# Two retimings in a matmul-bound kernel: the causal heads' value products after the gates' tile, the dilated heads' transposes without a wait

## The reference, cut to what matters

```
(qa, ka, va, za, qb, kb, vb, zb, qm, zm, gates) = split(h @ w_in)
qa, ka = rope(qa), rope(ka)                    # 8 causal heads of width 128
ya = softmax(qa ka^T / sqrt(128), causal) va * silu(za)
qb, kb = rope(qb), rope(kb)                    # 4 dilated heads, 3 dilations each
yb = mixture over the 3 dilations * silu(zb)
ym = softmax(qm mk^T / 16) mv * silu(zm)       # 4 memory heads of width 256
```

## Time and profile before

| | |
|---|---|
| Median of 3 runs | 3493.75 us (3493.48 to 3502.49) |
| Profiled execution | 3492.97 us, of which the span is 3491.7 us |
| PE busy | 3264.7 us, 93% of the span, 20298 matmuls |
| DVE busy, ACT busy | 1738.8 us (50%), 1260.3 us (36%) |
| A chunk's transfer, issue to landing | 4.2 us, median of 936 |
| Causal heads, dilated heads, memory heads | about 2458 to 2619 us, 2619 to 2893 us, 2893 to 3018 us of the span |

### The profile page before, as it was taken

How to read it: one execution, slowest core, us unless ns; L and a number is a source line. 1 busy time by engine, 2 the same in 40 slices (tenths; PEclk the granted TensorE clock), 3 DMA queues, 4 the chain that set the end, 5 groups by cost and what they waited for, 6 DMA issues and landing times.

```text
span 3491.7 us, 47726 instructions
## 1 busy us (share of the span) xinstructions
PE 3264.7 (93%) x20298; PEld 2782.5 (80%) x20298; DVE 1738.8 (50%) x2491; ACT 1260.3 (36%) x1779; POOL 0.2 (0%) x4
## 2 busy tenths in 40 slices
PE   5979999999999999999997988987999999999998
PEld 3757677777777777777866878876999998999998
DVE  4533243434334343433436667766666555555555
ACT  3432222222222222222224454444554444444443
POOL 0000000000000000000000000000000000000000
PEclk9989999999999999999998999998999999999999
DMA  7753433333332333323243324443545444466654
GB/s 302 285 186 145 171 117 116 105 127 121 109 129 101 109 103 127 127 103 133 97 144 122 115 97 133 133 133 115 172 148 167 151 150 165 151 196 194 195 188 151
DMA packets 141635, 508.93 MB, mean 146 GB/s; under 512 B 15344, under 2 KB 19568, under 8 KB 140656
## 3 DMA queue, kind: packets, MB, share of 16 engines
q1 hardware_dynamic: 137040, 493.03, 41.5%
q10 hardware_dynamic: 4384, 12.85, 1.0%
HBM read 501.62 MB, written 4.19 MB: 145 GB/s over the span
## 4 chain that ended last, share of the span: by engine, by line
PE 85%; DVE 6%; DMA 3%; ACT 3%; issue 2%; SPq 0%; ACTq 0%; DVEq 0%
PE bank L506 26%; PE bank L508 25%; PE bank L507 25%; DMA raw<-stream 3%; PE bank L559 2%; PE bank L672 2%; DVE w_lo L1413 1%; PE bank L757 1%; PE bank L738 1%; PE bank L658 1%; PE bank L674 1%; DVE a_rstd L1729 1%; ACT a_s L1169 1%; PE bank L748 0%; ACT w_hi L932 0%
## 5 line engine op out<-in xcount | busy, mean ns | idle before, releaser
L506 PE MATMUL bank<-h_hi,w_hi 128*128 128x256 f32 (+1 forms) x4032 | 1269.0, 315 | 23.9 <-DVE w_lo L1413 21.6
L1413 DVE TENSOR_TENSOR w_lo<-raw,w_hi 128x1024 fp32r<-128x1024 f32 x744 | 901.5, 1223 | 695.5 <-ACT w_hi L932 690.6
L507 PE MATMUL bank<-h_lo,w_hi 128*128 128x256 f32 (+1 forms) x4032 | 1244.7, 309 | 0.0
L508 PE MATMUL bank<-h_hi,w_lo 128*128 128x256 f32 (+1 forms) x4032 | 1244.7, 309 | 0.0
L932 ACT ACTIVATE w_hi<-raw 128x1024 fp32r<-128x1024 f32 x744 | 779.1, 1057 | 1059.5 <-PE bank L508 601.5
L506 PEld LDWEIGHTS bank<-h_hi,w_hi 128*128 128x128 f32 x4032 | 762.5, 189 | 92.5 <-issue 36.8
L507 PEld LDWEIGHTS bank<-h_lo,w_hi 128*128 128x128 f32 x4032 | 763.4, 189 | 46.6 <-issue 4.9
L508 PEld LDWEIGHTS bank<-h_hi,w_lo 128*128 128x128 f32 x4032 | 761.2, 189 | 43.6
L506 PE MATMUL bank<-w_hi,h_hi 128*128 128x512 f32 x704 | 288.4, 410 | 44.9 <-DVE w_lo L1413 40.6
L508 PE MATMUL bank<-w_hi,h_lo 128*128 128x512 f32 x704 | 279.5, 397 | 0.0
L507 PE MATMUL bank<-w_lo,h_hi 128*128 128x512 f32 x704 | 279.0, 396 | 0.0
(11 more groups left out here) (215 smaller groups left out, 2698.5 us busy)
## 6 DMA issues: line engine op xcount, KB each, us to landing
raw<-stream SPq DMA_DIRECT2D x936, 512.0 KB, 4.2
res<-tokens_in ACTq DMA_DIRECT2D x4, 1024.0 KB, 13.7
vg<-mem_in ACTq DMA_DIRECT2D x4, 512.0 KB, 10.7
res<-mem_kv ACTq DMA_DIRECT2D x2, 1024.0 KB, 10.0
out<-res SPq DMA_DIRECT2D x4, 512.0 KB, 3.0
mem_kv<-qk ACTq DMA_DIRECT2D x1, 1024.0 KB, 7.8
mem_kv<-vg ACTq DMA_DIRECT2D x1, 1024.0 KB, 11.1
tab<-tables ACTq DMA_DIRECT2D x1, 513.0 KB, 4.3
```

Source lines behind the costliest of these rows:

```text
L506: pe.matmul(out, sh, mh, start=start, stop=False)
L507: pe.matmul(out, sh, ml, start=False, stop=False)
L508: return pe.matmul(out, sl, mh, start=False, stop=stop)
L1413: dve.tensor_tensor(m.w_lo[slot][:, :], m.raw[SLOT[raw]][:, :], m.w_hi[slot][:, :].bitcast(F32), ALU.subtract).then_inc(s.lo, 1)
```

## The change

In the causal heads `moba_back` is cut in two. `moba_turns(h - 1)`, the transposes and their copy, stays where it was. `moba_outputs(h - 1)`, the products with the values and the first gating step, now follows the tile `mo_z`. The values have two buffers, `b_v[:, h % 2]`, and ACT fills the next one without waiting for the products of the head before. On ACT and DVE the splits for `mo_z` are issued ahead of the output step. The last causal head's transposes move in between the second and third key tile of the first dilated head. In the dilated heads PE no longer waits for the rotated keys ahead of the transposes. ACT still does.

```diff
 # PE
+    def moba_turns(h):
         transposes(("mo", h), m.b_s, L)
+    def moba_outputs(h):
         pe.wait_ge(*s["v_set"].at("mo", h))
-        outputs(("mo", h), [[m.b_v[:, 0, t, :] for t in range(2)]], m.b_pt, L)
+        outputs(("mo", h), [[m.b_v[:, h % 2, t, :] for t in range(2)]], m.b_pt, L)
...
         if h:
-            moba_back(h - 1)
+            moba_turns(h - 1)
         tile(("mo_z", h), LAT)
+        if h:
+            moba_outputs(h - 1)
         pe.wait_ge(*s["roped"].at("mo_q", h))
...
         for n in range(3):
             tile(("di_k", h, n), LAT)
+            if h == 0 and n == 1:
+                moba_turns(MOBA_HEADS - 1)
         if h:
-            pe.wait_ge(*s["roped"].at("di_k", h))
             dilated_turns(h - 1)
         else:
-            moba_back(MOBA_HEADS - 1)
+            moba_outputs(MOBA_HEADS - 1)
 # ACT
         if h:
-            moba_back(h - 1)
-            act.wait_ge(*s["pv"].at("mo", h - 1, 0))
+            moba_turns(h - 1)
         act.wait_ge(*banks.at("bv", 1, 1))
-        act.activation(m.b_v[:, 0, :, :], ...)
+        act.activation(m.b_v[:, h % 2, :, :], ...)
+        ahead(("mo_z", h))
         if h:
+            moba_outputs(h - 1)
             act.wait_ge(*s["y_lo"].at("mo", h - 1))
         tanh(("mo_z", h), m.b_g[:, 0, :])
...
             ahead(("di_k", h, n))
+            if h == 0 and n == 1:
+                moba_turns(MOBA_HEADS - 1)
         if h == 0:
-            moba_back(MOBA_HEADS - 1)
+            moba_outputs(MOBA_HEADS - 1)
 # DVE
+        ahead(("mo_z", h))
         if h:
             moba_back(h - 1)
         silu(("mo_z", h), m.b_g[:, 0, :])
```

More of the change, by code:

```diff
@@ L827, in tensor_program @@
             values_chunk(("bv", n), outs, c)
-    def moba_back(h):
+    def moba_turns(h):
         transposes(("mo", h), m.b_s, L)
+    def moba_outputs(h):
         pe.wait_ge(*s["v_set"].at("mo", h))
-        outputs(("mo", h), [[m.b_v[:, 0, t, :] for t in range(2)]], m.b_pt, L)
+        outputs(("mo", h), [[m.b_v[:, h % 2, t, :] for t in range(2)]], m.b_pt, L)
     def dilated_turns(h):
@@ L1304, in scalar_program @@
         if h:
-            moba_back(h - 1)
-            act.wait_ge(*s["pv"].at("mo", h - 1, 0))
+            moba_turns(h - 1)
         act.wait_ge(*banks.at("bv", 1, 1))
-        act.activation(m.b_v[:, 0, :, :], m.b_v_all[:, :, h * HEAD:(h + 1) * HEAD], ACT.Copy).then_inc(*s["v_set"].up("mo", h))
+        act.activation(m.b_v[:, h % 2, :, :], m.b_v_all[:, :, h * HEAD:(h + 1) * HEAD], ACT.Copy
+                       ).then_inc(*s["v_set"].up("mo", h))
+        ahead(("mo_z", h))
         if h:
+            moba_outputs(h - 1)
             act.wait_ge(*s["y_lo"].at("mo", h - 1))
```

## The result

The changed kernel takes 3460.01 us (median of 4 runs, 3458.26 to 3461.38), the kernel before beside it 3493.61. The ratio is 0.9894, 95% interval 0.9877 to 0.9912: 33.6 us faster by the medians. The forecast was 3457.5, range 3451 to 3468. The profiled execution has a span of 3459.3 us against 3491.7, 32.4 less.

What follows compares the result with a forecast made beforehand. PE was taken to bound the kernel, its chain being 85% PE. Gains of 12.9 (causal rounds), 0.8 (last causal head) and 22.4 (dilated heads) summed to 36.1 us, giving a median of 3457.5 us, range 3451 to 3468.

Steps and rivals of the forecast that it cites:

- the two waits: PE's longest in the stage: transposes on the rotation's last step, 15.5 us; products on ACT's copy of the transposes, 12.8.
- The causal rounds: Seven rounds on PE shrink from 20.38 to 18.51 us, 1.87 each, by start-to-start times; 13.1 before the ring's charge.
- The sum of 12.9: Causal rounds' total gain in us: 13.1 less 0.2 for the ring, with 9.9 and 13.9 as ends.
- The ring: ACT and DVE work once round a causal round: 18.77 us against PE's 18.51, lagging 1.6 in all.
- The 0.2 us that I charged for it: Causal rounds: of 1.6 us of ring lag, 1.4 is covered by the second query chunk's slack, 0.2 paid.
- The last causal head: Its idle 0.73 goes as a key tile hides the copy; gain 0.8 us, between 0.6 and 1.0.
- The dilated heads: Three stalls for the rotation go: 15.5 us idle plus 6.9 from the low clock behind them, 22.4 together.
- The forecast's 6.9: Dilated heads: half of 13.7 us run at half clock behind the stalls comes back.
- The rule of the Trainium skill: Dilated heads' clock penalty as throttled time times one minus the ratio: 3.4 us a stall, 10.2 in all; not used.
- The fourth chunk, just in time: Dilated heads: split ready at 2705.7 to 2706.0, PE wants it at 2706.3; costed at nothing, bound 1 us a head.
- the sum: Gains of causal rounds, last causal head and dilated heads: 12.9 + 0.8 + 22.4 = 36.1 us.
- one more or one less such stretch: A stall elsewhere meeting its low clock at another moment, some 1.7 to 3.4 us, counted in the range.

Runs made afterwards that it cites:

- after_again: The changed kernel run once more, nothing edited: 3457.58 us, ratio 0.9881 to the kernel before.
- causal_only: The changed kernel with PE's wait for the rotated keys put back ahead of the dilated heads' transposes: 3485.02 us, ratio 0.9975 to the kernel before.
- the filled stall: The kernel before with 40 matmuls nobody reads in each of the three dilated stalls, wait kept: 3493.66 us, ratio 0.9989 to the kernel before.
- ring_plus_1: The changed kernel with three unread copies, about 1 us, added on ScalarE behind the wait for y_lo in causal rounds 1 to 7: 3464.58 us.
- after_beside: The changed kernel, unedited, run beside a version that loads head 0's memory keys first: 3461.3 us, ratio 0.9912 to the kernel before.

## Why the prediction was right

**PE bounds the stage, and the two waits are worth their length.** Right: they went, nothing replaced them, and each part alone gave its share.

**The causal rounds, 1.87 each.** Right in mechanism and size. Where the key and query tiles run at the same pace as before, a round went from 20.38 to 18.52 or 18.54 (`after_again`, `causal_only`), 1.84 to 1.86. The start-to-start rows priced it, the idle 1.62 would have been too little. The sum of 12.9 came out as 11.4 because the changed kernel's trace had the slower pace in all seven rounds (18.93), the trace of before only in parts of three. Over all traces it is 12.3, and the forecast had no term for a pace that changes with the order.

**The ring.** Right: 18.70 against 18.77, and an added 1 us is paid only after three rounds. It fell behind in no trace of the changed kernel, as the rounds were 18.8 us or more on average. The 0.2 us that I charged for it was not paid.

**The last causal head.** 0.55 for 0.8, and the difference is pace again. Its first two key tiles took 11.50 us in the changed kernel and ran at the faster pace before, where two such tiles take 11.10. At like pace the gain is 0.95, the idle 0.73 and 0.2 of start-to-start saving. In the three traces where all of its tiles were slow the stretch took 62.11 us, 1.1 more than before.

**The dilated heads.** 15.5 of idle time gone, as said. The trace gave 24.8 in all, 2.4 over the 22.4, and the windows of the trace of before tell why. First the key tiles with the stall behind them (first and second round), then the query tiles behind the transposes (all three), then the query tiles of the changed kernel:

```profile
2680.10:2701.95 21.85, 16.68 (x147) 16.46 (x145) 15.15 (x19) 9.67 (x12) 0.00 (x0) 0.95 0.45 145
2750.24:2772.72 22.48, 17.31 (x146) 17.09 (x145) 15.18 (x19) 9.66 (x12) 0.00 (x0) 0.97 0.44 141
...
2704.42:2721.79 17.37, 17.37 (x147) 17.37 (x145) 8.20 (x8) 6.99 (x8) 0.00 (x0) 0.94 0.47 152
2775.19:2793.00 17.81, 17.81 (x147) 17.81 (x146) 8.21 (x8) 6.99 (x8) 0.00 (x0) 0.92 0.46 148
2846.40:2864.40 18.00, 18.00 (x146) 18.00 (x145) 8.21 (x8) 6.98 (x8) 0.00 (x0) 0.91 0.46 146
...
2688.31:2704.73 16.42, 16.42 (x147) 16.42 (x146) 10.53 (x11) 8.73 (x11) 0.00 (x0) 1.00 0.50 163
```

The transposes took 2.47 and now 1.23, three times: 3.7 us. The query tiles took 0.95, 1.39 and 1.58 us longer than 16.42, with the clock below 1.00: 3.9 us. So the clock was worth 7.6 us; the filled stall says 7.4. The forecast's 6.9 was somewhat small, because the windows of the earlier trace rows end before the clock is back at full. In the second and third round the key tiles ran at the slower pace besides, 1.3 us in all, and 0.15 a round is the run-out of the last matmul ahead of the wait, which the transposes now overlap. That makes 15.5 + 7.6 + 1.3 + 0.45 = 24.85. The rule of the Trainium skill ("TensorE: Matmul & The Clock Gate", Terms), throttled time times one half, would have given 10.2 for the clock. The trace does not agree with it here: of the 20.4 us at half clock PE was idle for nearly 5.

**The fourth chunk, just in time.** Right. DVE's rows in the changed kernel, the end of the rotation and the late splits:

```profile
2691.41 0.96 DVE L1486 TENSOR_TENSOR res<-res 128x768 f32<-128x768 f32 x1
2694.95 2.36 DVE L1424 TENSOR_TENSOR w_lo<-raw,w_hi 128x1024 fp32r<-128x1024 f32 x2 [2.59 <-ACT w_hi L937]
```

and ACT's, the three copies and the splits behind them:

```profile
2692.40 1.58 ACT L1181 ACTIVATE res<-bank 128x512 f32<-128x512 f32 x3 [2.96 <-DVE res L1486]
2693.85 4.05 ACT L937 ACTIVATE w_hi<-raw 128x1024 fp32r<-128x1024 f32 x4
```

The first of the two splits ends near 2696.2; PE, which begins the tiles at 2688.3, wants it after 8.3 us, at 2696.6. It leaves 0.4, the forecast had 0.3 to 0.6.

**What the sum left out** is the 4.4 us outside the stage. Its cause stays open. The clock could account for it in these two traces: the changed kernel's has 6.8 us more at half clock ahead of the causal heads, and behind the dilated ones 3.4 more, together worth up to 5.1 us. But a third trace speaks against the clock alone. From 60 us to the end of the first causal head's scores, `after_again` has 128 us at half clock, the first trace 123, and yet it gets there 4.2 us earlier. The windows around one such stretch, behind a stall that both kernels have near the end of the projections:

```profile
3352.00:3356.00 4.00, 2.08 (x19) 1.89 (x17) 2.17 (x4) 1.46 (x4) 0.00 (x0) 1.00 0.67 233
3356.00:3360.00 4.00, 3.62 (x21) 3.62 (x22) 1.55 (x2) 0.82 (x1) 0.00 (x0) 0.68 0.32 104
```

Before, the clock stayed at 1.00 behind that stall. The forecast's "one more or one less such stretch" was in the range, not in the sum. So the measured 3460.01, 2.5 us from the forecast, is a stage that gained 0.7 us more than was said and a loss elsewhere for which the sum had no term; by the medians of the other two chips the gain was 39.8 and 36.1 us. Within the stage, too, the errors cancel in part: the causal heads gave 1.8 us less than forecast, the dilated heads 2.4 more. One slip of arithmetic is in the sum: 36.1 below the median of 3493.75 is 3457.65, not 3457.5.

## What to carry to other kernels

Price a removed wait from start to start of the instructions on both sides, and look up the granted clock behind it: here 15.5 us of idle time were worth 23.6 at like pace. When an engine's step moves, follow the ring of the other engines' work once round and compare it with the bound engine's round; busy shares of 51% (ACT) and 70% (DVE) in a round said nothing of the two lines without which 8 us are lost. Before a few tenths of a per cent are explained, compare stretches that nobody changed.

## What the runs showed of the hardware

**TensorE runs the same matmuls at two paces at full clock.** Within an unbroken stretch of tile matmuls with 256 columns the distance from start to start is 113.3 ns or 117.8 ns, all through. In all traces looked at it changed at the switches between these and the float32 transposes, scores and products, or at a wait. It differs between executions of one kernel. The windows of one stretch that both kernels share, of `after_again` (which has 1.03 us of idle time at its end) and then `ring_plus_1`:

```profile
3019.00:3350.00 331.00, 329.97 (x2912) 329.77 (x2910) 188.41 (x222) 146.22 (x178) 0.00 (x0) 1.00 0.60 194
```

```profile
3019.00:3350.00 331.00, 331.00 (x2813) 331.00 (x2812) 182.64 (x214) 141.50 (x174) 0.00 (x0) 1.00 0.57 187
```

Both have a granted clock of 1.00; the second shows 99 matmuls fewer in the same 331 us. The projections have 3264 tile matmuls without a switch and 768 more behind one wait. At the slower pace that is 14.7 and 3.5 us. The profiled executions that had it there took 3481.1 us (`ring_plus_1`, others of its runs 3461 to 3470) and 3483.3 (`after_beside`, with both stretches slow, others from 3459). The runs of before above 3507 fit the same size, but no trace of one exists. What chooses the pace stays open. In the causal heads of the changed kernel the key and query tiles had the slower one in 13 of the 14 rounds of the first two traces, in others in turn.

**A stall's low clock moves with the moment.** Around the end of the wait of 5.4 us for `mem_kv` the clock was low for 3.4 us in the trace of before and 6.8 in that of the changed kernel, with the same idle time; up to 1.7 us of difference for nothing that was edited.
